# Expert-choice encoder layer: rank counts of experts 1 to 15 moved from VectorE to GpSimd and ScalarE, expert lists multiplied from bfloat16 pieces

## The reference

```python
logits = jnp.einsum('bsd,de->bse', h, w_router)
aff = jax.nn.softmax(logits, axis=-1)
gate, tok = lax.top_k(jnp.swapaxes(aff, 1, 2), cap)      # cap = 128 of 1024 tokens
xin = h[bidx, tok]
a = jnp.einsum('becd,edf->becf', xin, w_gate)
u = jnp.einsum('becd,edf->becf', xin, w_up)
y = jnp.einsum('becf,efd->becd', jax.nn.silu(a) * u, w_down)
y = y * gate[..., None]
return jnp.zeros_like(h).at[bidx, tok].add(y)
```

## Time and profile before

| what | value |
|---|---|
| median of 3 runs | 2771.25 us (2769.7 to 2777.27) |
| the profiled execution's own time | 2770.87 us |
| its span in the trace | 2768.8 us (2.07 us lie around it) |
| PE busy | 2684.0 us (97% of the span) |
| DVE busy | 2093.9 us (76%) |
| ACT busy | 1423.5 us (51%) |
| POOL busy | 485.6 us (18%) |
| mean granted TensorE clock | 0.985 |

### The profile page before, as it was taken

One profiled execution on the slowest core, in us unless ns is written; L12 is line 12 of the kernel. 1 busy time (PEld: TensorE's weight loads), 2 busy tenths in 40 slices (PEclk: granted clock), 3 DMA queues, 4 the chain that ended last, 5 costly groups with the idle time before them and its releaser, 6 DMA issues.

```text
span 2768.8 us, 33660 instructions
## 1 busy us (share of the span) xinstructions
PE 2684.0 (97%) x12353; PEld 2213.9 (80%) x12353; DVE 2093.9 (76%) x2787; ACT 1423.5 (51%) x1605; POOL 485.6 (18%) x746
## 2 busy tenths in 40 slices
PE   9999999999999999999999889999999999999996
PEld 7888888888888888788888777787777777777784
DVE  7775676587777667834375779888899889889987
ACT  6433221122322367733233466776777677777776
POOL 1432112211111446501010100111111001011001
PEclk9999999999999999999999999999999999999998
DMA  9688776898887785245353699999999999999998
GB/s 366 240 297 296 257 265 226 286 340 281 290 302 262 250 263 180 94 150 182 134 174 135 267 379 375 367 376 368 380 393 387 376 378 383 372 377 382 388 390 352
DMA packets 251123, 827.75 MB, mean 299 GB/s; under 512 B 30342, under 2 KB 55445, under 8 KB 227933
## 3 DMA queue, kind: packets, MB, share of 16 engines
q1 hardware_dynamic: 210528, 685.12, 66.3%
q0 software_dynamic: 40432, 140.49, 15.1%
HBM read 728.16 MB, written 99.91 MB: 299 GB/s over the span
## 4 chain that ended last, share of the span: by engine, by line
PE 79%; DVE 12%; ACT 3%; issue 2%; DMA 2%; POOL 1%; SPq 0%; ACTq 0%; DVEq 0%; POOLq 0%
PE ps L3210 14%; DVE elo L2674 8%; PE ps L2847 6%; PE ps L2846 6%; PE ps L2848 5%; PE ps L2842 5%; PE ps L2843 5%; PE ps L2844 5%; PE ps L3062 4%; PE ps L3064 4%; PE ps L3063 4%; PE ps L3241 4%; PE ps L3239 4%; PE ps L3240 4%; PE ps L2897 2%
## 5 line engine op out<-in xcount | busy, mean ns | idle before, releaser
L2674 DVE TENSOR_TENSOR elo<-eraw,ehi 128x2048 fp32r<-128x2048 f32 x384 | 873.6, 2290 | 123.6 <-ACT ehi L1785 114.8
L1785 ACT ACTIVATE ehi<-eraw 128x2048 fp32r<-128x2048 f32 x384 | 733.1, 1919 | 318.7 <-PE ps L3210 235.8
L1413 ACT ACTIVATE whi<-raw 128x1024 fp32r<-128x1024 f32 x159 | 168.6, 1060 | 577.8 <-PE ps L2848 246.2
L3210 PE MATMUL ps<-ehi,xh 128*128 128x512 f32 x960 | 384.0, 400 | 0.0
L3210 PE MATMUL ps<-elo,xh 128*128 128x512 f32 x960 | 381.5, 397 | 0.0
L1894 DVE TENSOR_TENSOR wlo<-raw,whi 128x1024 fp32r<-128x1024 f32 x159 | 194.6, 1224 | 185.1 <-ACT whi L1413 184.4
L3210 PE MATMUL ps<-ehi,xl 128*128 128x512 f32 x960 | 260.7, 394 | 0.0
L3210 PEld LDWEIGHTS ps<-ehi,xh 128*128 128x128 f32 x960 | 185.7, 193 | 38.8
L3210 PEld LDWEIGHTS ps<-elo,xh 128*128 128x128 f32 x960 | 185.5, 193 | 38.8
L3210 PEld LDWEIGHTS ps<-ehi,xl 128*128 128x128 f32 x960 | 183.3, 191 | 39.0
L3062 PE MATMUL ps<-ohi,a_hi 128*128 128x512 f32 x512 | 202.9, 396 | 0.9 <-DVE olo L2396 0.9
(11 more groups left out here) (496 smaller groups left out, 5503.0 us busy)
## 6 DMA issues: line engine op xcount, KB each, us to landing
raw<-in_w_stream SPq DMA_DIRECT2D x271, 512.0 KB, 5.0
eraw<-in_w_gate SPq DMA_DIRECT2D x256, 512.0 KB, 6.9
eraw<-in_w_up SPq DMA_DIRECT2D x256, 512.0 KB, 8.6
eraw<-in_w_down SPq DMA_DIRECT2D x128, 1024.0 KB, 7.7
oraw<-in_w_stream SPq DMA_DIRECT2D x128, 256.0 KB, 2.6
xt<-in_xT SPq DMA_DIRECT2D x48, 256.0 KB, 4.4
scr_ops<-xt POOLq DMA_DIRECT2D x48, 256.0 KB, 3.1
nav<-scr_rows SPq DMA_DIRECT2D x128, 64.0 KB, 4.0
```

The lines of the kernel that those rows point to most:

```text
L1413: act.activation(whi[:, c % SPL, :], raw_pair(c)[0], ACT.Copy).then_inc(S["w_hi"], 1)
L1785: act.activation(ehi[:, p % ERING, :], flat2(eraw[:, 2 * (p % EDEEP):2 * (p % EDEEP) + 2, :]), ACT.Copy)\
L2674: dve.tensor_tensor(elo[:, p % ERING, :], flat2(eraw[:, 2 * (p % EDEEP):2 * (p % EDEEP) + 2, :]), ehi[:, p % ERING, :].bitcast(F32), ALU.s ...
L3210: last = pe.matmul(gu_bank(e, c), a[:, k, :], w[:, p % ERING, c * BW:(c + 1) * BW], start=(k == 0 and a is hi and w is ehi), stop=(k == KD ...
```

## The change

The rank counts of experts 1 to 15 leave DVE. POOL compares (`compare`, now in POOL's program), without summing: it writes marks into `above`, 512 + 128 columns in bfloat16, two buffers. ACT sums them (`rank_sum`, an activation that also writes a sum, into `ranks`) at k = 3 to 6 of gu of expert e for expert e+1 (e = 0: k = 0 to 3), written as `SUMAT`. POOL then makes the four `place_hot`. Expert 0's counts stay on DVE. `list_products(e + 1)` moves from k = 7 to k = 9, `merge` from k = 8 to k = 10, `XTAT` from 11 to 13, `overlap` and `last_tokens` by two places. `place_hot` and `list_in` become bfloat16: the gate is held as three pieces, the token number as two (a multiple of 128 and the rest), so that the list has five columns. The pieces of the gate are split off on POOL (`split_gates`) instead of in one DVE instruction. `merge` sums two groups of columns and has seven instructions instead of six. At the start, POOL fetches row 1 ahead of `gather(0)`, and DVE splits pair 2 before the transposed tokens of expert 0.

```diff
+            def compare(e, n):
+                own, upto, turn, to = chosen[:, n, e:e + 1], n * P, 4 * (e - 1) + n, above[:, n % 2, :]
+                if n == 0:
+                    pool.wait_ge(S["row_in"], BEFORE["row_in"] + 16 * e)
+                    pool.wait_ge(S["listed"], BEFORE["listed"] + e)
+                if turn >= 2:
+                    pool.wait_ge(S["summed"], BEFORE["summed"] + turn - 1)
+                pool.tensor_scalar(out=to[:, upto:BW], in0=chances[:, upto:BW], scalar1=own, scalar2=None, op0=ALU.is_gt)                    .then_inc(S["compared"], 1)
+                if n:
+                    pool.tensor_scalar(out=to[:, 0:upto], in0=chances[:, 0:upto], scalar1=own, scalar2=None, op0=ALU.is_ge)                        .then_inc(S["compared"], 1)
+                pool.tensor_scalar(out=to[:, BW:BW + P], in0=chances[:, upto:upto + P], scalar1=own, scalar2=None, op0=ALU.is_equal)                    .then_inc(S["pool_step"], 1)
+                step.settle()
+                pool.tensor_tensor(to[:, BW:BW + P], to[:, BW:BW + P], lower[:, :], ALU.mult).then_inc(S["compared"], 1)
+
+            def place_ranks(e):
+                pool.wait_ge(S["summed"], BEFORE["summed"] + 4 * e)
+                for n in range(4):
+                    pool.tensor_scalar(out=place_hot[:, n, :], in0=countdown[:, :], scalar1=ranks[:, n:n + 1], scalar2=None,
+                                       op0=ALU.is_equal).then_inc(S["ranked"], 1)
+
+            fetch_row(1)
             gather(0)
+            rank(1)
             for e in range(1, NE):
-                fetch_row(e)
                 pool.wait_ge(S["xtr"], BEFORE["xtr"] + 4 * e)
                 if e >= 3:
                     add_outputs(e - 3)
                 gather(e)
+                if e + 1 < NE:
+                    rank(e + 1)
...
+            def rank_sum(e, n):
+                if n == 0:
+                    act.wait_ge(S["ranked"], BEFORE["ranked"] + 4 * e)
+                act.wait_ge(S["compared"], BEFORE["compared"] + MARKS * (e - 1) + 3 * n + 2)
+                act.activation(above[:, n % 2, :], above[:, n % 2, :], ACT.Copy, accum_out=ranks[:, n:n + 1]).then_inc(S["summed"], 1)
...
+                if kind == "gu" and e + 1 < NE and SUMAT[e > 0] <= k < SUMAT[e > 0] + 4:
+                    rank_sum(e + 1, k - SUMAT[e > 0])
...
-                    if e + 1 < NE and k == (6 if e == 0 else 7):
+                    if e + 1 < NE and k == (6 if e == 0 else 9):
                         list_products(e + 1)
```

More of the change, by code:

```diff
@@ L11 @@
 F32R = mybir.dt.float32r
+BF16 = mybir.dt.bfloat16
 U32 = mybir.dt.uint32
@@ L108 @@
 MARKS = 11
-XTAT = 11
+XTAT = 13
+SUMAT = (0, 3)
 FILLS = 12
@@ L274, in trunk @@
         picked.enter_context(nc.sbuf_tensor("under_places", [P, (224768 - ROOM) // 4], F32))
-        place_hot = sb("place_hot", [P, 4, P], F32R, picked)
-        chances = sb("chances", [P, BW], F32, picked)
+        place_hot = sb("place_hot", [P, 4, P], BF16, picked)
         picked.close()
@@ L2632, in merge @@
                 from_last, own = list_bank(e), slice(e, e + 1)
-                gate, ahead, apart = (merged[:, j:j + 1] for j in range(3))
+                gate, ahead, apart, token = (merged[:, j:j + 1] for j in range(4))
                 dve.wait_ge(S["listed"], BEFORE["listed"] + e + 1)
-                dve.tensor_reduce(out=gate, in_=from_last[:, 0:2], axis=AX.X, op=ALU.add).then_inc(S["dve_step"], 1)
-                dve.tensor_tensor(apart, first_token[:, own], from_last[:, 2:3], ALU.subtract).then_inc(S["dve_step"], 1)
+                dve.tensor_reduce(out=gate, in_=from_last[:, 0:3], axis=AX.X, op=ALU.add).then_inc(S["dve_step"], 1)
+                dve.tensor_reduce(out=token, in_=from_last[:, 3:5], axis=AX.X, op=ALU.add).then_inc(S["dve_step"], 1)
                 step.settle()
                 step.settle()
+                dve.tensor_tensor(apart, first_token[:, own], token, ALU.subtract).then_inc(S["dve_step"], 1)
                 dve.tensor_tensor(ahead, first_gate[:, own], gate, ALU.is_ge).then_inc(S["dve_step"], 1)
@@ L2642, in merge @@
                 step.settle()
-                dve.scalar_tensor_tensor(out=tokf[:, own], in0=apart, scalar=ahead, in1=from_last[:, 2:3], op0=ALU.mult, op1=ALU.add)\
+                step.settle()
+                dve.scalar_tensor_tensor(out=tokf[:, own], in0=apart, scalar=ahead, in1=token, op0=ALU.mult, op1=ALU.add)\
                     .then_inc(S["dve_step"], 1)
@@ L2663, in _ @@
             for n in range(4):
[L2664 to L2667, removed]
+                compare(n)
+            place_ranks()
             merge(0)
@@ L2706, in _ @@
                 dve.wait_ge(m, 64 * OHB // 2)
-            for p in range(2):
+            for p in range(3):
                 pair_low(p)
[L2709 to L2712, removed]
+            x_low(0, 0)
+            x_low(0, 1)
+            pair_low(3)
+            x_low(0, 2)
+            x_low(0, 3)
             for p in range(ERING, NP):
@@ L2722, in _ @@
                 if kind == "gu" and e + 1 < NE:
[L2723 to L2728, removed]
+                    if k == (7 if e == 0 else 10):
                         merge(e + 1)
-                if kind == "gu" and e == NE - 2 and k == 11:
+                if kind == "gu" and e == NE - 2 and k == 13:
                     overlap()
@@ L3165, in list_products @@
                     pe.wait_ge(S["ranked"], BEFORE["ranked"] + 4 * e + n + 1)
-                    last = pe.matmul(list_bank(e)[:, 0:4], place_hot[:, n, :], list_in[:, n, :, e], start=(n == 0), stop=(n == 3))
+                    last = pe.matmul(list_bank(e)[:, 0:5], place_hot[:, n, :], list_in[:, n, 0:5, e], start=(n == 0), stop=(n == 3))
                 last.then_inc(S["listed"], 1)
```

67 lines of the change are left out of this document (42 added, 25 removed).

## The result

The changed kernel took 2848.26 us (median of 4 runs, 2847.57 to 2849.33), beside 2772.23 for the kernel before: the ratio is 1.0272, its 95% interval [1.0254, 1.0290]. Forecast was 2714 us. The profiled execution took 2849.33 us, with a span of 2847.6 us, against a span of 2768.8 before: 78.8 us more.

The account below looks back on a forecast made before the run. PE was taken to set the pace, 2.72 us a pair, stopping for `place_hot` at lists. Stretches of 69.5 instead of 72.89 us, times 13, save 44 us, the start 13: 57 from 2770.87 gives 2714 us, range 2700 to 2730.

Parts of the forecast that it names:

- is `place_hot` in time?: Between ACT's sums and PE's list: one-hots end at 13.3 us after k = 3, PE due at 16.3, 3 us in hand.
- The price of a comparison: POOL's `compare`: 0.84 ns a column over 0.26 us, so 1.8 us for n = 2; dearest bound 3.6 ns a column.
- How POOL passes elo: POOL beside DVE's elo: two POOL instructions pass in each gap, since a 128-column one reads for about 0.1 of 0.37 us.
- Rival 1: POOL and DVE exclude each other; one POOL instruction passes per gap, PE waits 5.2 us at the list: 2816 us, chance 0.20.
- clock term of 3.0 us: Rival 1's dearest clock loss per stretch, added to 68.9 and the 5.2 us wait to give 77 us.
- the blocking is for the reading only: Argument against rival 1: elo blocks a POOL instruction only while it reads; ACT's stand also gives POOL room.
- The gain at the start: Before the thirteen stretches: 13.6 us from waits at expert 1 and lists 1 and 2 and clock, less 0.6: 13 us.
- The wait for expert 1's tokens: PE's one wait of 4.5 us near the start: goes, as `XTAT` two pairs later gives 5.4 us.
- Costs nothing: Side costs: scatter behind one-hots nothing; bfloat16 operands and gate splitting off the path, up to 0.5 us either way at list 0.
- The wait of 2.53 us: PE's stop for `place_hot` at each list; expected to go, as counts leave DVE, but for 0.6 us a stretch.
- Rival 2: Next limit met, DMA or ACT standing for comparisons: stretches stay near 71 us, 2733 us (2725 to 2760), chance 0.18.
- Rival 3: One-hots wait singly for elo, 2.7 us late at the list; stretches near 72.9 us, 2765 us; 0.07 with about no change.

Follow-up runs that it names:

- x3: The changed kernel with the four one-hots of each expert made by DVE instead of POOL; comparisons stay on POOL, sums on ACT: 2712.05 us.
- x9: The changed kernel with two of an expert's four one-hots left on POOL and the last two made by DVE: 2721.62 us.
- x1: The changed kernel with POOL's comparisons, triangle products and one-hots replaced by memsets of the same shapes, which read nothing: 2697.92 us.
- x4: The kernel before with only the bfloat16 lists and the gates in three pieces, list at its old place: 2772.93 us.
- x2: The kernel before with only the list later (k = 9 instead of 7, merge 10, `XTAT` 13), counts still on DVE: 2705.80 us.
- x6b: The changed kernel with POOL's comparisons and triangle products as memsets, so that only the one-hots read: 2798.63 us.
- x5: The changed kernel with the list products three pairs later (k = 12, merge 13): 2743.48 us.
- x10: The changed kernel with ACT's four sums three pairs earlier (k = 0 to 3), list unmoved: 2743.52 us.
- x7: The changed kernel with each pair's elo made by two DVE instructions of 1024 columns instead of one of 2048: 2799.57 us.

## Why the prediction was wrong, point by point

**The step that failed is "is `place_hot` in time?"** It had the last sum end at 11.8 and the one-hots at 13.3 us after PE's end of k = 3, PE being due at 16.3: 3 us in hand. On that clock (elapsed times of the trace, PE's k = 3 taken as 0.8 us before the ehi of the first sum, 2027.95) the first sum ends at 3.4, not 3.6; `compare` of n = 2 at 11.5, not 5.5; the last sum at 15.3, not 11.8; the one-hots at 24.5, not 13.3; and PE comes to the list at 17.2. Two errors are in it.

*The price of a comparison.* I took 0.84 ns a column over 0.26 us from the earlier trace rows. Unhindered, 128 columns take 0.61 us and 384 take 1.25: 2.5 ns a column over 0.29 us. That is within the bound I had named (3.6 ns) and harmless alone: `compare` of n = 3 is 2.9 us where I had 1.8.

*How POOL passes elo.* I chose two instructions to a gap, because a short one reads for little of its time. The rows show one to an elo where DVE's gap is 0.43 us: in the changed kernel 2.31, 2.73 and 2.43 us for the three comparisons of n = 2. Two one-hots got in at the gap of 0.56 us, and between back-to-back elos none until the second elo had gone. `compare` of n = 2 took 8.0 us and the one-hots 9.1, where I had 1.8 and 1.5; unhindered, by the rows above, they would be 2.9 and 2.4. So of 13.8 us too little, 2.0 are the price and 11.8 the passing. x3 and x9 show that the last two one-hots turn nearly all of it into time: on DVE instead, 2722 us, with all four there 2712.

One sum on the way doesn't come out, and enters neither the forecast nor the failure: the ehi may be 3.2 us late by the terms given (8.2 less 5.0), not 3.9.

**Rival 1 had the mechanism** and nearly its course: one instruction to an elo, ACT standing 3 us for `compare` of n = 2 (3.4 measured; by rival 1's own times, 12.5 less 8.2, it would have been 4.3), the gap that lets n = 3 through, the last sum "near 15" (15.3), the one-hots behind elo "without gaps". Its end was mis-sized: one-hots at 21.5 by one elo each, 24.5 by the trace, since the third waits for two; so a wait of 5.2 us was 6.8. Its clock term of 3.0 us holds: against x3's stretch of 68.62 the measured one of 78.39 has 9.8 us more, of which 6.8 are stops, leaving 2.9 us for the clock. A stretch was to be 77 and is 78.4. The thirteen gave 71.6 us more and not 55. Outside them I credited 10 us of gain, and 7 us were lost (the last list's own stop and clock alone cost 10). These 16.6 and 17 us bring 2816 to 2850, and the profiled execution took 2849. I gave it 0.20; the argument against it, "the blocking is for the reading only", had no row behind it, while the earlier trace rows had a POOL instruction of 0.54 us that took 2.33. The Trainium skill's rule in "SBUF — State Buffer", section "Who interferes with whom", that the two-input DVE instruction and the reading GpSimd instruction exclude each other, agrees with this: the one-hots took 2291 ns in the mean beside elo. x1, whose POOL instructions read nothing, goes free. The rule alone would hold a one-hot for one elo; the 4.52 us of the third, two elos, are more than it says, and the measurement decides.

**What held.** The other terms can be read in x3, which has all of the change but for four one-hots. A stretch: forecast 69.5 with 0.6 left at the list, measured 68.62; thirteen gain 55.5 us where I had 44. The gain at the start was forecast as 13 us. List 2 of x3 is reached 3.3 us earlier and, being two pairs (5.4 us) later in the program, that is 8.7. Against this its time behind list 15 is as long as before, 170.0 and 169.9 us, though two pairs shorter in work: a loss of 5.5 us for which the sum had no term. 4.1 us of it stand in one wait at the very end, POOL's for the DMA that writes `tiles_end` to `out`, 9.8 us where it was 5.7; why that came later isn't known. 2712 beside the forecast 2714 is thus luck, misses that cancel (11.5 us too little gain in the stretches, 4.3 and 5.5 too much outside them), and not a sum that was right in each term. The wait for expert 1's tokens went as forecast (4.5 us to 0.9). *Costs nothing* was right for the 16-bit lists (x4) and for the scatter behind POOL's one-hots, for which nothing in the stream of pairs waits.

**What I did not ask.** The wait of 2.53 us is shorter than a pair, 2.72. Moving the list later alone removes it, and x2 gives 2705.8 us. The sum credited the 2.53 us to the counts leaving DVE; the change's own second part, the list at k = 9, already pays for it, and the move of the counts only added a place where it could be lost. The prediction did not price the two halves apart.

**Rival 2** fell: x1 moves 407 GB/s and has stretches of 68.2 us at a DMA share of 1.02, no longer than PE's own work. **Rival 3** fell: the wait did not stay but grew. Its timing, one-hots passing elo singly with a last sum in time, is what x6b showed, and there the stops were 4.6 us and not 2.7: 74.99 us a stretch and 2799 us, where rival 3 had 2765.

Left open: why a stop of 2.5 us lowered the clock in some stretches of the kernel before and not in others, and what exactly makes a waiting POOL instruction miss the change between two back-to-back elos; no run varied the gap finely.

## What to carry to other kernels

Before work is moved off a busy engine to end a wait, compare the wait with the step of the schedule: a wait shorter than one step may go away by issuing the consumer later, with no work moved (x2: two pairs later, 66 us; one pair later was not run). Work given to GpSimd beside a stream of two-input VectorE instructions is priced by VectorE's instructions, not by its own length: count one per GpSimd instruction, two where they come back to back, and keep short GpSimd instructions off any path with a due time. And a producer that makes another engine late creates the backlog that later blocks it, so its delays can't be moved as a fixed block.

## What the runs showed of the hardware that was not expected

A GpSimd instruction that waits for VectorE is not served at the next end of a VectorE instruction if another one stands ready: a one-hot, 0.60 us unhindered, took 4.52 us in the changed kernel, from 0.45 us into one elo to 0.45 us after the start of the third. It was so in 15 of 60 one-hots there, in 29 of 60 in x5 and 27 of 60 in x10, and with half as long instructions (2.38 us for two of 1.2 us) in 30 of 60 in x7; in x6b, with 0.43 us between elos, never. The other side pays little: elo is 2336 ns in the mean, 2290 before.

```profile
L1392 POOL TENSOR_SCALAR place_hot<-countdown,ranks 128x128 bf16<-128x128 f32 x60 | 136.6, 2291 | 14.4 <-ACT above L1851 14.4
...
L1381 POOL TENSOR_SCALAR above<-chances,chosen 128x128 bf16<-128x128 f32 x15 | 9.1, 609 | 0.0
```

The same comparison of 128 columns takes 609 ns where DVE stands, and a one-hot of the same shape 2291 in the mean beside elo. GpSimd's memsets of these shapes are untouched beside the same elos: 204 to 208 ns for 128 columns in x6b.
